# Gate-vector product in column tiles, one term fewer at the inverse's start, a new order of cache values, page indices held in registers

## The reference

```python
h = rmsnorm(x, w['norm_mix'])
u = h @ w['w_in']
dn_qkv, dn_z, dn_b, dn_a, da_q, da_k, da_v, gate_a, gate_b = split_in(u)
...
# gated delta rule, in chunks of 64 tokens
beta = jax.nn.sigmoid(b_raw.astype(jnp.float32))
g = -jnp.exp(a_log) * jax.nn.softplus(a_raw + dt_bias)
M = A + jnp.eye(C, dtype=A.dtype)          # A strictly lower triangular, 64 x 64
X = lax.linalg.triangular_solve(M, rhs, left_side=True, lower=True, unit_diagonal=True)
...
# sample tokens: differential attention over paged keys and values
past_k = cache_k_l[page_table].reshape(DB, -1, DA_HEADS, 2 * DA_DH)
past_v = cache_v_l[page_table].reshape(DB, -1, DA_HEADS, DA_DV)
```

## Time and profile before

| | |
|---|---|
| median of three runs | 2774.84 us (2770.45 to 2776.49) |
| profiled execution, its own time | 2776.96 us |
| its span, first to last instruction | 2775.2 us |
| PE busy | 2724.4 us, 98% of the span |
| DVE, ACT, POOL busy | 1347.8, 1021.2, 241.1 us |
| mean granted TensorE clock | 0.992 |
| DMA moved | 304.61 MB, mean 110 GB/s |

### The profile page before, as it was taken

One profiled execution on the slowest core, in us unless ns is written; L12 is line 12 of the kernel. 1 busy time (PEld: TensorE's weight loads), 2 busy tenths in 40 slices (PEclk: granted clock), 3 DMA queues, 4 the chain that ended last, 5 costly groups with the idle time before them and its releaser, 6 DMA issues.

```text
span 2775.2 us, 56816 instructions
## 1 busy us (share of the span) xinstructions
PE 2724.4 (98%) x23886; PEld 2580.1 (93%) x23886; DVE 1347.8 (49%) x1662; ACT 1021.2 (37%) x1154; POOL 241.1 (9%) x148
## 2 busy tenths in 40 slices
PE   8999999999999999999999999999999999999997
PEld 8999999966599999999999999999656999999997
DVE  5333347644666533333653333557356755333336
ACT  5334224312553333322343332333135633333223
POOL 0111001321000011100001100012220000111000
PEclk9999999999999999999999999999999999999998
DMA  4222232267622322222322222322774222222221
GB/s 160 91 91 72 94 123 93 92 198 227 196 77 79 105 91 91 86 84 88 107 92 91 91 78 94 133 94 97 215 236 148 79 92 92 91 91 81 94 88 72
DMA packets 119537, 304.61 MB, mean 110 GB/s; under 512 B 14946, under 2 KB 24930, under 8 KB 118882
## 3 DMA queue, kind: packets, MB, share of 16 engines
q1 hardware_dynamic: 119394, 302.57, 33.1%
HBM read 291.08 MB, written 11.44 MB: 109 GB/s over the span
## 4 chain that ended last, share of the span: by engine, by line
PE 93%; DVE 3%; ACT 2%; DVEq 2%; issue 1%; DMA 0%; SPq 0%; POOLq 0%; ACTq 0%
PE ps L607 69%; PE ps L655 12%; PE ps L820 2%; PE ps L908 1%; PE ps L974 1%; ACT sc L1226 1%; PE ps L875 1%; PE ps L889 1%; PE ps L708 1%; PE ps L927 1%; PE ps L1124 1%; DVEq L1793 0%; PE ps L738 0%; PE ps L956 0%; DVEq L1985 0%
## 5 line engine op out<-in xcount | busy, mean ns | idle before, releaser
L607 PE MATMUL ps<-Hh,whi 128*128 128x260 f32 x3440 | 691.8, 282 | 11.3 <-DVE Hl L1719 9.8
L607 PE MATMUL ps<-Hl,whi 128*128 128x260 f32 x3440 | 690.1, 282 | 0.0
L607 PE MATMUL ps<-Hh,wlo 128*128 128x260 f32 x3440 | 689.0, 282 | 0.0
L1226 ACT ACTIVATE whi<-raw 128x2048 fp32r<-128x2048 f32 (+2 forms) x225 | 396.0, 1760 | 780.6 <-PE ps L607 670.0
L1653 DVE TENSOR_TENSOR wlo<-raw,whi 128x2048 fp32r<-128x2048 f32 (+2 forms) x213 | 444.2, 2086 | 291.2 <-ACT whi L1226 291.1
L607 PEld LDWEIGHTS ps<-Hh,whi 128*128 128x128 f32 x3440 | 527.9, 188 | 12.5 <-issue 9.7
L607 PEld LDWEIGHTS ps<-Hl,whi 128*128 128x128 f32 x3440 | 530.1, 189 | 0.0
L607 PEld LDWEIGHTS ps<-Hh,wlo 128*128 128x128 f32 x3440 | 529.2, 188 | 0.0
L1226 ACT ACT_TABLE_LOAD x163 | 209.1, 1283 | 303.8 <-PE ps L607 233.3
L1653 DVE TENSOR_TENSOR ta<-ps,R 128x520 f32<-128x520 f32 x88 | 61.6, 700 | 475.6 <-PE ps L607 474.5
L607 PE MATMUL ps<-Gh,whi 128*128 128x260 f32 x1408 | 284.0, 283 | 0.0
(11 more groups left out here) (283 smaller groups left out, 2980.5 us busy)
## 6 DMA issues: line engine op xcount, KB each, us to landing
raw<-in_ffn_up SPq DMA_DIRECT2D x176, 512.0 KB, 4.3
raw<-in_ffn_down SPq DMA_DIRECT2D x128, 352.0 KB, 3.3
kb<-in_cache_k SPq DMA_DIRECT2D x128, 256.0 KB, 3.1
kb<-in_cache_v SPq DMA_DIRECT2D x128, 256.0 KB, 3.1
raw<-in_w_in SPq DMA_DIRECT2D x56, 512.0 KB, 4.5
raw<-in_w_gate SPq DMA_DIRECT2D x32, 512.0 KB, 4.7
raw<-in_w_ab SPq DMA_DIRECT2D x16, 512.0 KB, 4.2
raw<-in_w_o SPq DMA_DIRECT2D x16, 512.0 KB, 4.5
```

The source lines that it names most:

```text
L607: last = nc.tensor.matmul(ps[:, bank + 2 * m + c, 0:HT], w, x[:, k0 + k, c * HT:(c + 1) * HT], start=starts and k == 0 and n == 0, stop=st ...
L1226: return nc.scalar.activation(out, in_, func, **kw)
```

## The change

Four edits. (1) The gate vectors: the weight block keeps 32 columns instead of 128, ACT multiplies it by the norm's gain in 8 instructions into `wbg`, and PE multiplies it with `X` itself, in plain fp32, in 16 matmuls of 32 weight columns: four of the eight k tiles stand side by side in the four column groups of the array, and their four partial sums are added when `BA` (now 128 rows) is turned with the constant `C_FOLD` instead of the identity. POOL's `wbal` is gone. (2) The inverse: POOL adds the identity to level 0 (one more instruction for each G, after a drain), and PE's two identity matmuls for each G are gone. (3) The order of values is a table. (4) Page indices: 48 of 64 are read once for a layer, 12 after each of the loads of blocks 48 to 51, held in registers, and used for keys and values; the 16 others (the first four tiles of keys, and the values of the same pages) are read at each use.

```diff
-        wba = s0.sb("wba", [P, KD, P])
-        wbah = s0.sb("wbah", [P, KD, P], R32)
-        wbal = s0.sb("wbal", [P, KD, P], R32)
-        BA = s0.sb("BA", [2 * H, T])
+        wba = s0.sb("wba", [P, KD, 32])
+        wbg = s0.sb("wbg", [P, KD, 32])
+        BA = s0.sb("BA", [P, T])
...
+        PAGES_HELD = [s * NPAGE + h * 4 + g for h in range(2) for s in range(NSEQ) if h or s > 3 for g in range(4)]
+        VALUES = (0, 1, 1, 2, 1, 0, 1, 2, 1, 0, 1, 2, 1, 0, 0, 1, 1, 1)
...
-                pg = sp_.value_load(pages[0:1, s * NPAGE + half * 4 + g:s * NPAGE + half * 4 + g + 1],
-                                    min_val=0, max_val=A["cache_v"].shape[1] - 1)
+                n = s * NPAGE + half * 4 + g
+                pg = known[n] if n in known else page_index(sp_, n)
...
-                seq(L, B_IN + 10, B_IN + 14)
+                known = {}
+                for n in range(4):
+                    seq(L, B_IN + 10 + n, B_IN + 11 + n)
+                    known.update((m, page_index(sp_, m)) for m in PAGES_HELD[n * len(PAGES_HELD) // 4:(n + 1) * len(PAGES_HELD) // 4])
...
-                pe.wait_ge(t_pool.sem, t_pool.at("w", L))
+                pe.wait_ge(t_act.sem, t_act.at("w", L))
                 pe.wait_ge(evac, L * NE + (37 + FREE))
-                for k in range(KD):
-                    for n, (w, x) in enumerate(((wbah, Hh), (wbah, Hl), (wbal, Hh))):
-                        for c in range(2):
-                            last = nc.tensor.matmul(ps[:, 4 + c, 0:HT], w[:, k, :], x[:, k, c * HT:(c + 1) * HT],
-                                                    start=k == 0 and n == 0, stop=k == KD - 1 and n == 2)
+                for k in range(KD // 4):
+                    for c in range(2):
+                        for g in range(4):
+                            last = nc.tensor.matmul(ps[32 * g:32 * g + 32, 4 + c, 0:HT], wbg[:, 4 * k + g, :],
+                                                    X[:, 4 * k + g, c * HT:(c + 1) * HT], start=k == 0, stop=k == KD // 4 - 1)
...
-                        turned(b, (6, slice(n * 8, n * 8 + 8)), BA[:, n * CH:(n + 1) * CH], 8)
-                tr(ps[0:NSEQ, 6, 64:72], BA[:, SEQ:T], 8).then_inc(t_pe.on("tok", L), 1)
+                        nc.tensor.matmul(ps[part(b), 6, n * 8:n * 8 + 8], BA[:, n * CH:(n + 1) * CH], CC[:, C_FOLD:C_FOLD + 2 * H],
+                                         start=True, stop=True)
+                nc.tensor.matmul(ps[0:NSEQ, 6, 64:72], BA[:, SEQ:T], CC[:, C_FOLD:C_FOLD + 2 * H], start=True, stop=True
+                                 ).then_inc(t_pe.on("tok", L), 1)
...
-                    nc.tensor.matmul(flat(ps[:, UB[G], :]), ident, rows(M_I64), start=True, stop=False, skip_group_check=True)
-                    nc.tensor.matmul(ps[:, UB[G], :], ident, n0, start=False, stop=False, skip_group_check=True
+                    nc.tensor.matmul(ps[:, UB[G], :], ident, n0, start=True, stop=False, skip_group_check=True
                                      ).then_inc(d_pe.on(f"u0{G}", L), 1)
-                    nc.tensor.matmul(flat(ps[:, TB[G], :]), ident, rows(M_I64), start=True, stop=False, skip_group_check=True)
-                    cells(TB[G], n0, lambda r, c: CM[r, M_I64:M_I64 + CH], False, False).then_inc(d_pe.on(f"t0{G}", L), 1)
+                    cells(TB[G], n0, lambda r, c: CM[r, M_I64:M_I64 + CH], None, False).then_inc(d_pe.on(f"t0{G}", L), 1)
...
-                    elif i < 14:
-                        value(i - 1)
-                    elif i > 14:
-                        value(i - 2)
+                    for j in range(sum(VALUES[0:i]), sum(VALUES[0:i + 1])):
+                        value(j)
...
-                A_(wbah[:, :, :], wba[:, :, :], ACT.Copy).then_inc(t_act.on("w", L), 1)
+                for k in range(KD):
+                    last = A_(wbg[:, k, :], wba[:, k, :], ACT.Copy, scale=gain(L, 1, k))
+                last.then_inc(t_act.on("w", L), 1)
...
+                    if l == 0:
+                        pool.drain()
+                        last = nc.gpsimd.tensor_tensor(flat(NTl[:, G, 0, :]), flat(NTl[:, G, 0, :]), rows(M_I64), ALU.add)
```

More of the change, by code:

```diff
@@ L43 @@
 NEG = -1.0e30
-C_ID, C_ONE, C_SLOPE, C_LI, C_OML, C_EPS, NCC = 0, 128, 256, 260, 262, 264, 266
+C_ID, C_ONE, C_SLOPE, C_LI, C_OML, C_EPS, C_FOLD, NCC = 0, 128, 256, 260, 262, 264, 266, 274
 B_UP1, B_IN, B_GATE, B_O, B_UP2, B_PLE, NB = 0, 38, 52, 64, 68, 106, 112
@@ L77, in core_constants @@
     c[:, C_EPS] = EPS
+    c[:, C_FOLD:C_FOLD + 2 * H] = np.arange(P)[:, None] % 32 == np.arange(2 * H)
     return c
@@ L399, in hybrid_trunk, with page_index, cache_pages @@
         block = ctx.enter_context(nc.Block())
-        def cache_pages(sp_, cache, L, t):
+        def page_index(sp_, n):
+            return sp_.value_load(pages[0:1, n:n + 1], min_val=0, max_val=A["cache_v"].shape[1] - 1)
+        def cache_pages(sp_, cache, L, t, known):
             s, half = (t % NSEQ, t // NSEQ) if t < 16 else ((t - 16) // 2, t % 2)
             for g in range(4):
-                pg = sp_.value_load(pages[0:1, s * NPAGE + half * 4 + g:s * NPAGE + half * 4 + g + 1],
-                                    min_val=0, max_val=A["cache_v"].shape[1] - 1)
+                n = s * NPAGE + half * 4 + g
+                pg = known[n] if n in known else page_index(sp_, n)
                 sp_.dma_start(kb[t % 4][:, g, :], cache[L, bass.ds(pg, 1)].rearrange("o p c -> p (o c)")
@@ L475, in _ @@
                 sp_.dma_start(O["conv_old"][L], scin[:, :, 8:24]).then_inc(tail_out, 16)
-                seq(L, B_IN + 10, B_IN + 14)
+                if L == 0:
+                    sp_.wait_ge(late_loads, 32)
+                known = {}
+                for n in range(4):
+                    seq(L, B_IN + 10 + n, B_IN + 11 + n)
+                    known.update((m, page_index(sp_, m)) for m in PAGES_HELD[n * len(PAGES_HELD) // 4:(n + 1) * len(PAGES_HELD) // 4])
                 sp_.wait_ge(evac, L * NE + 42 + FREE)
@@ L481, in _ @@
                 sp_.wait_ge(block_done, L * NB + (B_GATE - 1 + FREE))
-                if L == 0:
-                    sp_.wait_ge(late_loads, 32)
                 for t in range(2):
-                    cache_pages(sp_, A["cache_k"], L, t)
+                    cache_pages(sp_, A["cache_k"], L, t, known)
                 sp_.wait_ge(split_done, L * NB + (B_GATE - 1 + FREE))
@@ L500, in _ @@
                     sp_.wait_ge(q_pe.sem, q_pe.at(f"k{t - 4}" if t < 20 else f"v{t - 20}", L))
-                    cache_pages(sp_, A["cache_v"], L, t)
+                    cache_pages(sp_, A["cache_v"], L, t, known)
                     if t == 19:
@@ L820, in cells @@
                             last = nc.tensor.matmul(ps[part(h % 2), bank, cell(x, h)], lhs[part(h % 2), cell(x, h)],
-                                                    rhs(part(h % 2), cell(x, h)), start=start, stop=stop, skip_group_check=True)
+                                                    rhs(part(h % 2), cell(x, h)), start=x == 0 and h < 2 if start is None else start,
+                                                    stop=stop, skip_group_check=True)
                     return last
@@ L1598, in _ @@
                 ffn(L, 0, 0)
-                pool.wait_ge(t_act.sem, t_act.at("w", L))
-                nc.gpsimd.tensor_tensor(wbal[:, :, :], wba[:, :, :], wbah[:, :, :].bitcast(F32), ALU.subtract
-                                        ).then_inc(t_pool.sem, 1)
                 pool.wait_ge(split_done, L * NB + (46 + FREE))
@@ L1613, in mask @@
                         pool.wait_ge(d_dve.sem, d_dve.at(f"nt{G}", L))
-                    nc.gpsimd.tensor_tensor(flat(NTl[:, G, l % 2, :]), flat(NT[:, G, :]), rows(M_ML + CH * l), ALU.mult
-                                            ).then_inc(d_pool.on(f"m{l}{G}", L), 1)
+                    last = nc.gpsimd.tensor_tensor(flat(NTl[:, G, l % 2, :]), flat(NT[:, G, :]), rows(M_ML + CH * l), ALU.mult)
+                    if l == 0:
+                        pool.drain()
+                        last = nc.gpsimd.tensor_tensor(flat(NTl[:, G, 0, :]), flat(NTl[:, G, 0, :]), rows(M_I64), ALU.add)
+                    last.then_inc(d_pool.on(f"m{l}{G}", L), 1)
                 def decay(b):
@@ L1811, in _ @@
                 dve.wait_ge(t_pe.sem, t_pe.at("ba", L))
-                TT(halves(BA[:, :]), ps[0:2 * H, 4:6, 0:HT], halves(R[0:2 * H, :]), ALU.mult).then_inc(t_dve.on("ba", L), 1)
+                TT(halves(BA[:, :]), ps[:, 4:6, 0:HT], halves(R[:, :]), ALU.mult).then_inc(t_dve.on("ba", L), 1)
                 low_u(2)
```

3 lines of the change are left out of this document (1 added, 2 removed).

## The result

The changed kernel takes 2758.2 us in the median of 5 executions (2755.79 to 2758.85), the kernel before 2774.15 us in the same comparison (2770.45 to 2776.49): ratio 0.9944, 95% interval 0.9931 to 0.9957, 16 us less. The forecast was 2755.0. The profiled execution took 2756.83 us with a span of 2755.0, against 2776.96 and 2775.2 before: 20.2 us less from span to span. The two differences, 16 and 20, are the question that is left, and the experiments come back to it.

What follows compares the result with a forecast made beforehand. PE was taken to bound the kernel, busy 98% and 93% of the chain. Terms of 3.56 + 3.55 + 2.97 = 10.1 us a layer, 20.2 for both, took 2774.84 to 2755 us, range 2748 to 2766.

Steps and rivals of the forecast that it cites:

- Gate vectors: Product of 5.76 us a layer becomes 2.1, turning 0.1 longer: net 3.56 us less a layer.
- that rival (0.07): At the gate vectors, column groups do not overlap: 7.0 us instead of 2.1, giving 2764 us; chance 0.07.
- The rule on column tiling: At the gate product, column tiling disables fast weight load; if loads were the limit, 17.4 us saved instead of 20.2.
- Inverse: First step of the inverse: four fp32 matmuls off PE, 3.55 us less a layer; POOL's addition costs nothing.
- Values: Attention loop: three value tiles a layer move into PE's pauses at i = 3, 7, 11, 2.97 us less a layer.
- The pause: PE's idle 1.05 us at i = 3 takes a second value free; rival that it is not: 2760.5 us, chance 0.08.
- Page indices: SP's queue: faster page transfers give 0 by themselves, but cover PE coming about 3.6 us sooner to the last key tile.
- 0.42 us: Sign in the changed profile: page DMAs on SP's queue 0.42 us apart, against 1.11 us before.
- the rival on the clock (0.20): Mixers: another share of half clock; one more 7 us stretch a layer gives 6.2 us back, 2761 us; chance 0.20.
- half clock for more than about 7 us in a mixer: Sign that the forecast is wrong: the clock stays at half for more than about 7 us in a mixer.

Runs made afterwards that it cites:

- `gate_serial`: The changed kernel with the 32 passes of its gate-vector product ordered group by group, so neighbouring passes share the same 32 array columns: 2761.75 us, ratio 0.9958.
- `values_only`: The kernel before with the order of the value tiles alone changed: 2770.68 us, ratio 0.9983.
- `pages_only`: The kernel before with only the page indices of 48 of 64 pages read ahead and held: 2775.33 us, ratio 0.9998.
- `no_pages`: The changed kernel without its page-index edit, each index read just ahead of its transfer for both caches: 2763.08 us, ratio 0.9957.

## Why the prediction was right

**Gate vectors: right.** Forecast 3.56 us a layer. The chain shows 5.76 to 1.91 less 0.04 of turning, 3.8. The price by the key tile's row, 0.99 us for eight passes of 512 columns in four groups, came within 0.2 us. `gate_serial` shows the overlap of groups to be the reason, and that rival (0.07) is out. The rule on column tiling that I weighed (Trainium skill, TensorEngine Tiling, Restrictions) did not set the time: 1.91 us is far below the 3.5 us of 32 loads in a row, so the loads of 109 ns are hidden when the groups alternate. Whether column tiling made a load longer is not shown, since the key tiles with their 109 ns are column tiled too.

**Inverse: right, with the clock as its uncertainty.** Forecast 3.55. Without half clock the stretch from key to scores is 75.3 us with the old inverse and 71.8 with the new one, 3.4 for the edit, and a stretch of half clock adds about 3 to either. I had assumed that such a stretch stays in its place, and it did not: it is 3.4 us shorter or away, and there is more of it ahead of the heads. POOL's addition is hidden, as said.

**Values: right.** Forecast 2.97. `values_only` has 2.97 and 2.95 in its heads' stretch, and the wait for the scores' tile falls from 10.8 to 5.7 us for 6 tiles moved. The pause was free to 0.19 us.

**Page indices: right alone, and the cover was the point.** I counted 0 and wrote that the edit covers the second one. `pages_only` gives 0; `no_pages` puts 5.6 us on the cover, with a lower clock as a part of it. The step that was missing is this number: I had said that PE comes 3.6 us sooner to the last key tile, from a spare of 1.3 to 4.5 us, and drew no price from it. The page DMAs came closer than before but not to 0.42 us: four of them take 1.95 us, (1.95 - 0.33) / 3 = 0.54 apart.

```profile
633.03 1.95 SPq L411 DMA_DIRECT2D kb<-in_cache_k  x4
```

**The sum.** The four terms give 20.2. The profiled spans differ by 20.2 too, but that is luck: 23.5 less in the mixers, of which some 2 are clock (27 us of the mixers stand at half clock before and 24 now, by the clock's records in the two traces), and 3.3 more in code that did not change, most of it the slower start of that execution. The medians differ by 16.0 and 17.6 in the two comparisons. Where do 3 us go? Each execution comes with its mean granted clock. A core at half clock for t us does t/2 us of work less, so (1 - clock) x time is what the clock can have cost at most. Over the 34 executions of before the mean is 0.9937, 17.5 us; over the ten of the changed kernel 0.9925, 20.7 us. The means of the times differ by 17.9 us; with the clock's share taken off, 2757.8 and 2736.6 are left, about 21 us apart. By the same count the single edits are worth 6.7 (gate), 7.5 (inverse), 5.7 (values) and 0.1 us (pages), 20.0 together, against terms of 7.1, 7.1, 5.9 and 0. The full price may not apply: among the 34 executions, the three at 0.991 took 2779.9 us in the mean and the five at 0.996 took 2771.6, 8.3 us for 13.9 us of lost clock, 0.6 of it. By that the changed kernel lost 1.9 us more to the clock, and the sum would be 19.8. Either way the work taken off is what the terms say, and the changed kernel stands a little longer at half clock than the old one. That is an account from clocks that are given to 0.001, 2.8 us a step, and that leave out the start of the kernel. It is not an experiment.

So the rival on the clock (0.20) happened in its longer form, at about half its size: I had it as one more stretch a layer, 6.2 us. I had also named "half clock for more than about 7 us in a mixer" as what would make the forecast wrong. There is such a stretch in the changed profile, 657 to 671 us at 0.51. The forecast held because another stretch had gone. What stays open is why the clock falls at the inverse and ahead of the heads, and why a little more in the changed kernel. PE is busy 13.66 of 14.00 us there. The long stretch ahead of the heads does not come from the change alone: `pages_only`, which takes the time of before, has one as well, with a clock of 0.52 from 661 to 675 us and PE busy for 13.66 us of it. Emptied pauses make the clock fall elsewhere, which is shown; nothing was tried on the narrow products themselves.

## What to carry to other kernels

Work that a busy engine does in the waits of another chain is worth its full length on either side of the move, and on PE it also holds up the clock: here emptied pauses cost 15.6 us through the clock, for 6 us of work taken out of them. An edit that is worth nothing alone may be the cover of another one, so work out the spare that the other one eats, and try the change without it. Products with few output rows should alternate between column groups in program order; one group after another costs more than twice the time.

## What was not expected of the hardware

- Three throwaway products of about 1 us a layer saved 15.6 us, since the granted clock stayed at 1.00 where it had fallen to 0.66 and 0.57 (layer 0) and 0.51 (layer 1) behind pauses of 2.0 to 2.4 us.
- The same program has its half clock in different places from one execution to the next: at 597 to 604 us the clock was 0.86 in one profile of the changed kernel and 1.00 in the other.
- Neighbouring 260-column passes in four column groups cost 0.060 us each, and 0.143 us in one group, with weight loads of 109 and 110 ns.
- A read of a page index, doubled between weight loads, cost at most 0.56 us, and 36 more of them in 44 us of the queue did not hold up a single block.
- The thirteen profiles, with the same work of PE up to the first gate product, reach it between 484.7 and 487.6 us; the later ones run their first matmuls at half speed for up to 6 us longer, which the recorded clock does not show.
